# Feed-forwards whose up products read rows not yet normed, with the inverse root multiplied in at the banks

## The chip, the cores and the metric

The kernel runs on one core of a Trainium2 chip. The metric is the device time of one execution in microseconds, the median of several runs. The engines are named as the profile names them: PE (TensorE, matrix products), PEld (its weight loads), DVE (VectorE), ACT (ScalarE), POOL (GpSimd) and SP (SyncE, which issues the weight transfers).

## What is computed

Three residual blocks, one after the other, on 512 rows of width 1024. Each ends in a feed-forward of hidden width 2816 (the second block has two of them). All is float32. The part that matters here:

```python
# first block (second block: silu, centred convolution)
hf = rmsnorm(x, norm_ffn[i])
up = causal_dwconv(hf @ w_up[i], ffn_dw_w[i], ffn_dw_b[i])     # width 3, per channel
gate, val = jnp.split(up, 2, axis=-1)
x = x + (jax.nn.gelu(gate) * val) @ w_down[i]
# third block: no norm ahead, no convolution
ffn = (jax.nn.silu(x @ w_ffn_gate) * (x @ w_ffn_up)) @ w_ffn_down
x = _layernorm(ALPHA * x + ffn, ln2_g, ln2_b)
# rmsnorm(x, g) = x * rsqrt(mean(x * x) + eps) * g, over the width
```

## The kernel before

The residual `G.x` lies in SBUF transposed: 8 tiles (KT) of 128 channels by 512 rows. `feed_forward` (line 210) is called four times: `ffn1`, `ffn2` and `ffn3` with a gain (they norm first) and taps (a convolution of width 3 along the rows), `ffn4` with neither. Every call is a stage of its own: the engines meet before and after it.

**Products.** `exact_product` (line 189) makes a float32 product of three passes over operands split into a rounded high part and the rest as a low part: w_low by x_high, w_high by x_low, w_high by x_high, lines 192 to 194. So both weights and rows have to be split. ACT makes a high part with a copy into fp32r (`high`, line 311, for weights; line 322 for rows), then the low part is the difference: POOL does it for weights (`low`, line 255), DVE for rows (line 365).

**Up part.** Weights come in chunks of 4096 columns per partition through a ring of two slots; a chunk is split in two halves of 2048. A half h of chunk (p, i) gives one gate tile and one value tile of the hidden width, so there are 22 halves, t = 4i + 2p + h. For each half PE does 2 tiles x 8 k x 3 passes = 48 matmuls of 128x512 into two of the eight banks (`up`, line 271): half t uses banks 4p + 2h and the next one, so banks come round again after four halves. `split` counts finished weight halves. The split parts have room for two halves: ACT may make the high part of half t + 2 only when PE is done with half t (`gate_val`), and POOL follows.

**After each half** ACT (lines 324 to 342) first makes that next high part, then two centre taps from the banks with bias (`gc`, `vc`, lines 333 and 335). DVE adds the two side taps to each, reading bank and buffer (line 383, four instructions), ACT applies the activation on the gate (line 338), and DVE multiplies gate by value into `gT` (line 397). The second side taps also set the banks free.

**Entry, with a gain.** `rms_act` (line 144) squares the 8 tiles into `gT`, PE sums them with a matrix of ones into bank 7 (`rms_pe`, 8 products), DVE forms the mean, ACT the root, DVE the reciprocal and the normed rows into `G.hT` (`rms_dve`, lines 166 to 171), ACT and DVE split those 8 tiles, and PE's first product waits for the first of them (`h_split`). Between its squares and the root ACT makes the high parts of halves 0 and 1.

**Down part.** The 22 hidden tiles are split by ACT (line 350) and DVE (line 405) and multiplied with the down weights. Its first product waits for the last bank, for tile 0's split and for the first down weights.

SP loads the next chunk when POOL has split both halves of one (`G.feed` on `split`). `pairs` (line 52) puts the halves of two chunks into one hardware loop on each engine.

## Time and profile before

| | us |
|---|---|
| median of 3 runs | 4812.88 |
| the runs | 4821.88, 4768.9, 4812.88 |
| the profiled execution | 4808.09 |
| its span, first to last instruction | 4806.3 |
| mean granted clock of PE | 0.941 of full speed |

All durations below come from the one profiled execution. A line of the timeline gives the start in us from the span's start, the duration, the engine, the line of the code and, in square brackets, how long the engine sat idle before it and what released it. A line that ends in x8 stands for eight instructions in a row, and its duration is from the start of the first to the end of the last; neighbouring instructions on ACT, DVE and PE overlap a little, so start to start is less than a single duration. Matmul ends are modelled; their starts are what counts.

### The profile page before, as it was taken

What the parts mean: (1) busy time and instruction counts of PE and PEld (TensorE: products, weight loads), DVE (VectorE), ACT (ScalarE), POOL (GpSimd) and SP (SyncE); (2) the same over time, 40 slices, a digit from 0 to 9 for tenths busy, and PEclk for the clock granted to TensorE, in tenths of its full rate; (3) what the DMA queues carried; (4) which work ended last, traced back from release to release, by engine and by line L of the source; (5) the groups of instructions that cost most, each with busy time, mean ns of one, the idle gap of its engine ahead of it and who ended that gap; (6) DMA issues with size and microseconds to landing.
All of it is one profiled execution on the core that took longest, in us unless ns stands there. A gap on an engine that the chain in (4) does not pass through costs nothing. (4 is left out here: it accounts for less than half of the span.)

```text
span 4806.3 us, 55253 instructions
## 1 busy us (share of the span) xinstructions
PE 4393.2 (91%) x22216; PEld 3404.0 (71%) x22216; DVE 2163.0 (45%) x3645; ACT 1362.3 (28%) x2087; POOL 1272.1 (26%) x474
## 2 busy tenths in 40 slices
PE   8999899978989998979999989989998887987998
PEld 6766587734747875668888668757776775765876
DVE  5543333335643345457777533444552436122023
ACT  3343244212203423323333334322222111102222
POOL 1000343301203430000000134334554332653432
PEclk9996999988999999889999999999999998998999
DMA  5200122211112222421000212221211110211221
GB/s 166 105 36 18 70 87 105 92 70 70 70 53 87 98 93 91 158 101 36 21 34 21 72 53 105 88 76 60 81 70 67 60 53 36 88 70 70 103 90 53
DMA packets 41294, 357.92 MB, mean 74 GB/s; under 512 B 4275, under 2 KB 4659, under 8 KB 21500
## 3 DMA queue, kind: packets, MB, share of 16 engines
q1 hardware_dynamic: 41084, 354.97, 20.4%
q8 instruction: 150, 2.46, 0.2%
q14 instruction: 60, 0.49, 0.0%
HBM read 333.46 MB, written 21.50 MB: 74 GB/s over the span
## 5 line engine op out<-in xcount | busy, mean ns | idle before, releaser
L255 POOL TENSOR_TENSOR ffn_weights_low<-weight_ring,ffn_weights_high 128x2048 fp32r<-128x2048 f32 x132 | 615.0, 4660 | 1140.8 <-ACT ffn_weights_high L311 1140.8
L192 PE MATMUL banks<-ffn_in_high,ffn_weights_low 128*128 128x512 f32 x2112 | 829.6, 393 | 92.5 <-DVE ffn_in_low L365 61.8
L193 PE MATMUL banks<-ffn_in_low,ffn_weights_high 128*128 128x512 f32 x2112 | 827.7, 392 | 0.0
L194 PE MATMUL banks<-ffn_in_high,ffn_weights_high 128*128 128x512 f32 x2112 | 826.8, 391 | 0.0
L192 PEld LDWEIGHTS banks<-ffn_in_high,ffn_weights_low 128*128 128x128 f32 x2112 | 400.4, 190 | 181.2 <-issue 67.1
L194 PEld LDWEIGHTS banks<-ffn_in_high,ffn_weights_high 128*128 128x128 f32 x2112 | 400.1, 189 | 84.2
L193 PEld LDWEIGHTS banks<-ffn_in_low,ffn_weights_high 128*128 128x128 f32 x2112 | 400.5, 190 | 83.1
L311 ACT ACTIVATE ffn_weights_high<-weight_ring 128x2048 fp32r<-128x2048 f32 x132 | 252.4, 1915 | 655.4 <-PE banks L194 654.9
L192 PE MATMUL banks<-third_x_high,third_weights_low 128*128 128x512 f32 x832 | 333.5, 401 | 61.5 <-POOL third_weights_low L3011 24.2
L3011 POOL TENSOR_TENSOR third_weights_low<-weight_ring,third_weights_high 128x1024 fp32r<-128x1024 f32 x144 | 361.1, 2508 | 11.5
L3009 POOL CAST third_weights_high<-weight_ring 128x1024 fp32r<-128x1024 f32 x144 | 157.4, 1093 | 653.4 <-PE banks L194 488.2
L193 PE MATMUL banks<-third_x_low,third_weights_high 128*128 128x512 f32 x832 | 329.8, 396 | 0.0
L194 PE MATMUL banks<-third_x_high,third_weights_high 128*128 128x512 f32 x832 | 329.3, 396 | 0.0
L383 DVE SCALAR_TENSOR_TENSOR ffn_gate<-banks,columns_sb,ffn_gate 128x511 f32<-128x511 f32 (+1 forms) x132 | 98.4, 745 | 481.9 <-ACT ffn_value L335 481.9
L2794 POOL TENSOR_TENSOR rwout_weights_low<-weight_ring,rwout_weights_high 128x1024 fp32r<-128x1024 f32 x8 | 18.8, 2384 | 904.0 <-ACT rwout_weights_high L2844 904.0
L405 DVE TENSOR_TENSOR ffn_in_low<-ffn_hidden,ffn_in_high 128x512 fp32r<-128x512 f32 x88 | 172.1, 2004 | 178.7 <-ACT ffn_in_high L350 178.6
L192 PEld LDWEIGHTS banks<-third_x_high,third_weights_low 128*128 128x128 f32 x832 | 160.3, 193 | 99.5 <-DVE third_x_low L3668 17.7
L193 PEld LDWEIGHTS banks<-third_x_low,third_weights_high 128*128 128x128 f32 x832 | 160.1, 192 | 33.7 <-issue 0.7
L194 PEld LDWEIGHTS banks<-third_x_high,third_weights_high 128*128 128x128 f32 x832 | 159.7, 192 | 34.2
L192 PE MATMUL banks<-first_in_high,first_weights_low 128*128 128x512 f32 x336 | 145.8, 434 | 15.5 <-DVE first_in_low L847 12.3
L3262 DVE SCALAR_TENSOR_TENSOR mlstm_conv<-mlstm_z,columns_sb,mlstm_conv 128x512 f32<-128x512 f32 x96 | 134.8, 1404 | 3.4
L193 PE MATMUL banks<-first_in_low,first_weights_high 128*128 128x512 f32 x336 | 136.3, 406 | 0.0
(541 smaller groups left out, 7813.4 us busy)
## 6 DMA issues: line engine op xcount, KB each, us to landing
weight_ring<-weights SPq DMA_DIRECT2D x144, 2048.0 KB, 7.7
scan_in<-rwkv_operands SPq DMA_DIRECT2D x8, 1280.0 KB, 6.6
rwkv_operands<-rwin_staged SPq DMA_DIRECT2D x24, 256.0 KB, 2.1
scan_in<-rwkv_operands SPq DMA_DIRECT2D x8, 512.0 KB, 3.9
bias_tiles<-bias_rows SPq DMA_DIRECT2D x8, 448.0 KB, 9.1
residual<-x SPq DMA_DIRECT2D x4, 512.0 KB, 7.3
filt_decay<-decay SPq DMA_DIRECT2D x1, 2048.0 KB, 8.6
rwkv_residual<-residual SPq DMA_DIRECT2D x1, 2048.0 KB, 7.1
```

Source lines behind the costliest of these rows:

```text
L192: pe.matmul(out, w[1], x[0], start=start, stop=False, skip_group_check=True)
L193: pe.matmul(out, w[0], x[1], start=False, stop=False, skip_group_check=True)
L194: return pe.matmul(out, w[0], x[0], start=False, stop=stop, skip_group_check=True)
L255: pool.tensor_tensor(parts[1], landed, parts[0].bitcast(F32), ALU.subtract).then_inc(S["split"], 1)
L311: act.activation(parts[0], landed, ACT.Copy).then_inc(S["rounded"], 1)
L383: ins = dve.scalar_tensor_tensor(out=buf[:, h, to], in0=G.banks[:, b + q, of], scalar=G.col(taps, 8 * t + 4 * q + tap), in1=buf[:, h, to], ...
L405: dve.tensor_tensor(h_parts[1][:, t % KT, :], gT[:, t, :], h_parts[0][:, t % KT, :].bitcast(F32), ALU.subtract)\
L2794: pool.tensor_tensor(w_parts[1][:, k, :], landed(k), w_parts[0][:, k, :].bitcast(F32), ALU.subtract).then_inc(S["split"], 1)
L3009: pool.tensor_copy(parts[0], landed).then_inc(S["rounded"], 1)
L3011: pool.tensor_tensor(parts[1], landed, parts[0].bitcast(F32), ALU.subtract).then_inc(S["split"], 1)
L3262: ins = dve.scalar_tensor_tensor(out=cv[:, m, :], in0=of, scalar=G.col("m_conv", at + tap), in1=cv[:, m, :], op0=ALU.mult, op1=ALU.add)
```

## The change

In the stages with a gain the up products no longer wait for the norm. They read x times gain, split into high and low; since the inverse root is one number per row, it can be multiplied in after the product. DVE does that for each half: two `tensor_tensor` from the banks by `rstd` into a new SBUF buffer `up_scaled`, and these also set the banks free. Centre taps and side taps then read `up_scaled` instead of the banks. The squares, their sum (now seven additions on DVE and one product with the ones on PE instead of eight), the mean, root and reciprocal run beside the first halves; PE does the one product between the two tiles of half 1. In all four stages the first half's weights are split in eight pieces of 128x256, one per k, in turn with the row tiles; PE takes half 0 with k outside and the two tiles inside, waiting for each piece. Loops of POOL, PE and ACT are cut differently, as half 0 and (on ACT) the first and last chunks stand outside. The diff, its core:

```diff
         gT = G.sb(name + "_hidden", [P, FT, SEQ], ctx=ctx)
-        sq = gT[:, 0:KT, :]
+        sq, square_sum = gT[:, 0:KT, :], gT[:, KT, :]
         rstd = G.sb(name + "_rstd", [P, SEQ], ctx=ctx)
-
+        up_scaled = G.sb(name + "_up", [P, 2, 2, SEQ], ctx=ctx)
         gc = G.sb(name + "_gate", [P, 2, SEQ], ctx=ctx)
         vc = G.sb(name + "_value", [P, 2, SEQ], ctx=ctx)
         w_parts = [G.sb(name + "_weights_" + part, [P, 2, half], F32R, ctx=ctx) for part in ("high", "low")]
-
-        h_parts = [G.sb(name + "_in_" + part, [P, KT, SEQ], F32R, ctx=ctx) for part in ("high", "low")]
-        of = G.x if gain is None else G.hT
+        x_parts = [G.sb(name + "_in_" + part, [P, KT, SEQ], F32R, ctx=ctx) for part in ("high", "low")]
...
+        def pairs_from_one(eng, count, body):
+
+            assert count % 2
+            body(0, 0)
+            with eng.Fori(0, count // 2) as i:
+                body(1, i)
+                body(0, i + 1)
...
                 landed, parts = landed_half(p, h, up)
-                pool.wait_ge(S["rounded"], 4 * i + 2 * p + h + 1)
+                pool.wait_ge(S["rounded"], 4 * i + 2 * p + h)
                 pool.tensor_tensor(parts[1], landed, parts[0].bitcast(F32), ALU.subtract).then_inc(S["split"], 1)
...
+            landed, parts = landed_half(0, 0, True)
+            for k in range(KT):
+                pool.wait_ge(S["piece_high"], k + 1)
+                pool.tensor_tensor(parts[1][:, k, :], landed[:, k, :], parts[0][:, k, :].bitcast(F32), ALU.subtract).then_inc(S["piece_split"], 1)
+            pool.wait_ge(S["piece_split"], KT)
+            pool.sem_inc(S["split"], 1)
+            pairs_from_one(pool, UP_CHUNKS, chunk)
...
+                    t = 4 * i + 2 * p + h
+
+                    def product(m, k):
+                        return exact_product(pe, G.banks[:, 4 * p + 2 * h + m, :], [x[:, k, m * P:(m + 1) * P] for x in w],
+                                             [x[:, k, :] for x in x_parts], start=(k == 0), stop=(k == KT - 1))
+
+                    if first and h == 0:
+                        for k in range(KT):
+                            pe.wait_ge(S["piece_split"], k + 1)
+                            pe.wait_ge(S["x_split"], k + 1)
+                            for m in range(2):
+                                mm = product(m, k)
+                                if k == KT - 1:
+                                    mm.then_inc(S["gate_val"], 1)
+                        continue
+                    pe.wait_ge(S["split"], t + 1)
                     for m in range(2):
-
-                        pe.wait_ge(S["value_free"] if conv and m else S["gate_free"], 4 * i + 2 * p + h + 1)
+                        pe.wait_ge(S["value_scaled"] if m else S["gate_scaled"], t + 1)
+                        if gain is not None and p == h == m == 1:
+                            pe.wait_ge(S["mean_done"], 1)
...
+                            mm = product(m, k)
                         mm.then_inc(S["gate_val"], 1)
-
-            pairs(pe, UP_CHUNKS, up)
+                        if first and gain is not None and m == 0:
+                            pe.wait_ge(S["square_added"], KT - 1)
+                            pe.matmul(G.banks[:, 7, :], G.con("ones"), square_sum, start=True, stop=True).then_inc(S["summed"], 1)
+
...
+            landed, parts = landed_half(0, 0, True)
+            G.arrived(act, 0, 0)
+            for k in range(KT):
+                act.activation(parts[0][:, k, :], landed[:, k, :], ACT.Copy).then_inc(S["piece_high"], 1)
+                if gain is None:
+                    act.activation(x_parts[0][:, k, :], G.x[:, k, :], ACT.Copy).then_inc(S["x_high"], 1)
+                else:
+                    act.activation(x_parts[0][:, k, :], G.x[:, k, :], ACT.Identity, scale=G.col(gain, k)).then_inc(S["x_high"], 1)
+                if k == KT // 2:
+                    high(0, 0, 1, True)
             if gain is not None:
-                rms_act(act, G, S, sq)
-            for h in range(2):
-                high(0, 0, h, True)
-            if gain is not None:
-                rms_root(act, G, S, rstd)
-            for k in range(KT):
-                if gain is not None:
-                    act.wait_ge(S["h_ready"], k + 1)
-                act.activation(h_parts[0][:, k, :], of[:, k, :], ACT.Copy).then_inc(S["h_high"], 1)
+                for k in range(KT):
+                    act.activation(sq[:, k, :], G.x[:, k, :], ACT.Square).then_inc(S["squared"], 1)
 
             def chunk(p, i):
                 for h in range(2):
                     t = 4 * i + 2 * p + h
                     b = 4 * p + 2 * h
-                    act.wait_ge(S["gate_val"], 8 * i + 4 * p + 2 * h + 2)
+                    act.wait_ge(S["gate_val"], 2 * t + 2)
                     high(1 - p, i + p, h, isinstance(i, int) is False or 2 * i + p + 1 < UP_CHUNKS)
+                    if gain is not None and isinstance(i, int) and p == i == h == 0:
+                        rms_root(act, G, S, rstd)
 
                     act.wait_ge(S["hidden"], t + 1)
                     if conv:
-                        act.activation(gc[:, h, :], G.banks[:, b, :], ACT.Identity, bias=G.col(taps, 8 * t + 3),
+                        act.wait_ge(S["gate_scaled"], 4 + t + 1)
+                        act.activation(gc[:, h, :], up_scaled[:, h, 0, :], ACT.Identity, bias=G.col(taps, 8 * t + 3),
                                        scale=G.col(taps, 8 * t + 2 - shift)).then_inc(S["centre"], 1)
-                        act.activation(vc[:, h, :], G.banks[:, b + 1, :], ACT.Identity, bias=G.col(taps, 8 * t + 7),
+                        act.wait_ge(S["value_scaled"], 4 + t + 1)
+                        act.activation(vc[:, h, :], up_scaled[:, h, 1, :], ACT.Identity, bias=G.col(taps, 8 * t + 7),
                                        scale=G.col(taps, 8 * t + 6 - shift)).then_inc(S["centre"], 1)
-                        act.wait_ge(S["gate_free"], 4 + t + 1)
+                        act.wait_ge(S["gate_tapped"], t + 1)
                         act.activation(gc[:, h, :], gc[:, h, :], act_func).then_inc(S["activated"], 1)
                     else:
...
+            chunk(0, 0)
+            with act.Fori(0, UP_CHUNKS // 2 - 1) as i:
+                chunk(1, i)
+                chunk(0, i + 1)
+            chunk(1, UP_CHUNKS // 2 - 1)
+            chunk(0, UP_CHUNKS // 2)
...
+            for k in range(KT):
+                dve.wait_ge(S["x_high"], k + 1)
+                high = x_parts[0][:, k, :].bitcast(F32)
+                if gain is None:
+                    dve.tensor_tensor(x_parts[1][:, k, :], G.x[:, k, :], high, ALU.subtract).then_inc(S["x_split"], 1)
+                else:
+                    dve.scalar_tensor_tensor(out=x_parts[1][:, k, :], in0=G.x[:, k, :], scalar=G.col(gain, k), in1=high,
+                                             op0=ALU.mult, op1=ALU.subtract).then_inc(S["x_split"], 1)
             if gain is not None:
-                rms_dve(dve, G, S, rstd, 7, gain, G.hT)
-            for k in range(KT):
-                dve.wait_ge(S["h_high"], k + 1)
-                dve.tensor_tensor(h_parts[1][:, k, :], of[:, k, :], h_parts[0][:, k, :].bitcast(F32), ALU.subtract).then_inc(S["h_split"], 1)
+                for k in range(1, KT):
+                    dve.wait_ge(S["squared"], k + 1)
+                    if k > 1:
+                        dve.wait_ge(S["square_added"], k - 1)
+                    dve.tensor_tensor(square_sum, sq[:, 0, :] if k == 1 else square_sum, sq[:, k, :], ALU.add).then_inc(S["square_added"], 1)
+                dve.wait_ge(S["summed"], 1)
+                dve.tensor_scalar(rstd[:, :], G.banks[:, 7, :], 1.0 / D, EPS, ALU.mult, ALU.add).then_inc(S["mean_done"], 1)
+                dve.wait_ge(S["root_done"], 1)
+                dve.reciprocal(rstd[:, :], rstd[:, :]).then_inc(S["rstd_done"], 1)
+                dve.wait_ge(S["rstd_done"], 1)
...
+                        for q, free in enumerate((S["gate_scaled"], S["value_scaled"])):
+                            dve.wait_ge(S["gate_val"], 2 * t + q + 1)
+                            dve.tensor_tensor(up_scaled[:, h, q, :], G.banks[:, b + q, :], rstd[:, :], ALU.mult).then_inc(free, 1)
                         dve.wait_ge(S["centre"], 2 * t + 2)
                         for s, (tap, to, of) in enumerate(sides):
                             for q, buf in enumerate((gc, vc)):
                                 if s == 1:
                                     dve.wait_ge(S["tap"], 2 * t + q + 1)
                                 ins = dve.scalar_tensor_tensor(
-                                    out=buf[:, h, to], in0=G.banks[:, b + q, of], scalar=G.col(taps, 8 * t + 4 * q + tap),
+                                    out=buf[:, h, to], in0=up_scaled[:, h, q, of], scalar=G.col(taps, 8 * t + 4 * q + tap),
                                     in1=buf[:, h, to], op0=ALU.mult, op1=ALU.add)
                                 if s == 0:
                                     ins.then_inc(S["tap"], 1)
                                 else:
-                                    ins.then_inc((S["gate_free"], S["value_free"])[q], 1)
+                                    ins.then_inc((S["gate_tapped"], S["value_tapped"])[q], 1)
                         dve.wait_ge(S["activated"], t + 1)
-                        dve.wait_ge(S["value_free"], 4 + t + 1)
-                        value = vc[:, h, :]
+                        dve.wait_ge(S["value_tapped"], t + 1)
+                        dve.tensor_tensor(gT[:, t, :], gc[:, h, :], vc[:, h, :], ALU.mult).then_inc(S["hidden"], 1)
...
```

## Rows read from the trace of the kernel before

**Rows 1.** The page, busy time of each engine over the whole span

```profile
PE 4393.2 (91%) x22216; PEld 3404.0 (71%) x22216; DVE 2163.0 (45%) x3645; ACT 1362.3 (28%) x2087; POOL 1272.1 (26%) x474
```

**Rows 2.** Timeline, PE and ACT, entry of `ffn1`: start us, us, engine, line

```profile
558.89 0.39 PE L194 MATMUL banks<-first_in_high,first_weights_high 128*128 128x512 f32 x1
560.30 4.27 ACT L147 ACTIVATE ffn_hidden<-residual 128x512 f32<-128x512 f32 x8 [43.54 <-PEq L1106]
...
581.42 0.77 PE L192 MATMUL banks<-ffn_in_high,ffn_weights_low 128*128 128x512 f32 x1 [13.31 <-DVE ffn_in_low L365]
```

**Rows 3.** Timeline, ACT, POOL and DVE between those rows

```profile
564.47 3.70 ACT L311 ACTIVATE ffn_weights_high<-weight_ring 128x2048 fp32r<-128x2048 f32 x2
566.45 9.04 POOL L255 TENSOR_TENSOR ffn_weights_low<-weight_ring,ffn_weights_high 128x2048 fp32r<-128x2048 f32 x2 [14.43 <-ACT ffn_weights_high L311]
568.16 0.69 DVE L166 TENSOR_SCALAR ffn_rstd<-banks 128x512 f32<-128x512 f32 x1 [8.15 <-PE banks L159]
569.48 0.63 ACT L152 ACTIVATE ffn_rstd<-ffn_rstd 128x512 f32<-128x512 f32 x1
570.15 3.35 DVE L168 RECIPROCAL ffn_rstd<-ffn_rstd 128x512 f32<-128x512 f32 x1 [1.30 <-ACT ffn_rstd L152]
573.54 2.50 DVE L171 SCALAR_TENSOR_TENSOR normed<-residual,columns_sb,ffn_rstd 128x512 f32<-128x512 f32 x1
```

**Rows 4.** Timeline, ACT, its first instruction after halves 0, 1 and 3

```profile
594.10 1.28 ACT L311 ACT_TABLE_LOAD   x1 [12.76 <-PE banks L194]
...
604.92 1.92 ACT L311 ACTIVATE ffn_weights_high<-weight_ring 128x2048 fp32r<-128x2048 f32 x1 [3.38 <-PE banks L194]
...
626.68 1.92 ACT L311 ACTIVATE ffn_weights_high<-weight_ring 128x2048 fp32r<-128x2048 f32 x1 [4.64 <-PE banks L194]
```

**Rows 5.** Timeline, all engines, last up half of `ffn1` to first down product

```profile
822.09 0.39 PE L194 MATMUL banks<-ffn_in_high,ffn_weights_high 128*128 128x512 f32 x1
822.51 1.91 ACT L311 ACTIVATE ffn_weights_high<-weight_ring 128x2048 fp32r<-128x2048 f32 x1 [4.87 <-PE banks L194]
...
824.50 4.57 POOL L255 TENSOR_TENSOR ffn_weights_low<-weight_ring,ffn_weights_high 128x2048 fp32r<-128x2048 f32 x1 [6.20 <-ACT ffn_weights_high L311]
...
825.79 0.75 DVE L383 SCALAR_TENSOR_TENSOR ffn_gate<-banks,columns_sb,ffn_gate 128x510 f32<-128x510 f32 x1 [6.95 <-ACT ffn_value L335]
...
827.89 0.63 ACT L338 ACTIVATE ffn_gate<-ffn_gate 128x512 f32<-128x512 f32 x1 [2.13 <-DVE ffn_gate L383]
...
828.62 1.00 DVE L397 TENSOR_TENSOR ffn_hidden<-ffn_gate,ffn_value 128x512 f32<-128x512 f32 x1
...
830.32 0.76 PE L192 MATMUL banks<-ffn_in_high,ffn_weights_low 128*128 128x512 f32 x1 [7.84 <-issue]
```

**Rows 6.** Timeline, entry of `ffn4`, ACT, POOL and DVE

```profile
4386.55 3.71 ACT L311 ACTIVATE ffn_weights_high<-weight_ring 128x2048 fp32r<-128x2048 f32 x2 [0.28 <-PEq L3700]
...
4393.06 5.08 POOL L255 TENSOR_TENSOR ffn_weights_low<-weight_ring,ffn_weights_high 128x2048 fp32r<-128x2048 f32 x1
4393.57 5.12 DVE L365 TENSOR_TENSOR ffn_in_low<-residual,ffn_in_high 128x512 fp32r<-128x512 f32 x1
...
4422.65 1.92 ACT L311 ACTIVATE ffn_weights_high<-weight_ring 128x2048 fp32r<-128x2048 f32 x1 [5.69 <-PE banks L194]
```

**Rows 7.** One line's instructions: duration ns min/median/max, forms

```profile
L1131 POOL TENSOR_TENSOR first_weights_low<-weight_ring,first_weights_high x8: 2372/2429/2430, 482.7 to 549.6; 128x1024 fp32r<-128x1024 f32 x8
```

**Rows 8.** Timeline, PE, first product after an idle time of 2.41 and 4.25 us

```profile
155.79 0.50 PE L192 MATMUL banks<-first_in_high,first_weights_low 128*128 128x512 f32 x1 [2.41 <-DVE first_weights_low L872]
...
4152.16 0.77 PE L192 MATMUL banks<-third_x_high,third_weights_low 128*128 128x512 f32 x1 [4.25 <-DVE third_x_low L3668]
```

**Rows 9.** Timeline, DVE and POOL in the first stage of the kernel

```profile
28.21 3.69 DVE L847 TENSOR_TENSOR first_in_low<-normed,first_in_high 128x512 fp32r<-128x512 f32 x6
...
28.77 5.43 POOL L622 TENSOR_TENSOR first_weights_low<-weight_ring,first_weights_high 128x1024 fp32r<-128x1024 f32 x1 [6.87 <-ACT first_weights_high L751]
```

**Rows 10.** The page, costliest groups: busy us, mean ns of one, idle before

```profile
L3262 DVE SCALAR_TENSOR_TENSOR mlstm_conv<-mlstm_z,columns_sb,mlstm_conv 128x512 f32<-128x512 f32 x96 | 134.8, 1404 | 3.4
```

40 lines of the change are left out of this document (17 added, 23 removed).

## Prediction

> **What bounds the kernel now.** First the busy times of the page: PE works 91% of the span [rows 1], so a change pays only where it closes a gap of PE or shortens its stream. Next the timeline of PE where a feed-forward begins: the last product of the stage before starts at 558.89 and the first up product at 581.42 [rows 2]; only the eight products with the ones lie between. That is 22.5 us of mostly idle PE; from ACT's first instruction, 560.30, to that product it is 21.1 us, and `ffn2` and `ffn3` repeat this within 0.1 us, two entries more of the same kind. Third, what fills it [rows 3]: squares, two high parts of weights, mean (568.16), root (569.48), reciprocal (570.15, 3.35 us), then the normed rows from 573.54, then their split. Fourth, when halves end: ACT is free and waits for PE, so its first instruction after a half marks the end: 594.10, 604.92, 626.68 for halves 0, 1 and 3 [rows 4]. A half at full rate takes (626.68 - 604.92) / 2 = 10.9 us, 0.226 us for each of 48 matmuls; half 0 takes 12.7, the 1.8 us more being the low clock after a long idle time. Last the joint to the down part, 822.09 to 830.32 [rows 5]: another gap, in which a chain over ACT, POOL and DVE sets the end.
>
> **The port, which decides most of this.** At 573.54 DVE starts an instruction with two SBUF inputs that takes 2.50 us [rows 3]; POOL's subtraction, also two SBUF inputs, ends at 566.45 + 9.04 = 575.49, and DVE 0.55 later. The same in `ffn4`: 5.12 us for a subtraction [rows 6]. But the side tap at 825.79, with one input in a bank, takes 0.75 us in the middle of POOL's 4.57 [rows 5]. So a DVE instruction with both tensors in SBUF waits for POOL's to end, and one that reads a bank does not. The change moves the side taps' source from banks to SBUF and adds seven additions of that kind. The Trainium skill, SBUF — State Buffer, section "Who interferes with whom", says that a DVE instruction with two SBUF inputs blocks against a GpSimd one that reads SBUF, for the whole instruction, which speaks against such a move; the trace agrees (2.50 us beside 0.75). Taken as bandwidth shared or as nothing, the sum would be rival C's; taken as a lock it is the one below.
>
> **Entry of ffn1 to ffn3, from ACT's first instruction (0 = 560.30 [rows 2]).** Before: first product 21.1, half 0 ends 33.8, half 1 44.6, half 3 66.4 [rows 2, 4].
>
> Half 0. ACT now alternates a piece of 128x256 and a row tile. 512 columns take 0.53 from start to start (4.27 / 8, [rows 2]) and 2048 take 1.85 (3.70 / 2, [rows 3]), so 256 take 0.3, a pair 0.9, and eight pairs with half 1's high part 9.1 us: ACT isn't the limit. A POOL piece isn't in the trace: 1024 columns take 2.43 [rows 7], 2048 take 4.57 [rows 5], so a straight line through the two gives 0.8 for 256, which I take; bounds are 0.57 (an eighth of 4.57) and 1.2 (half of 2.43). The low part of the rows is DVE with two SBUF inputs, 0.66. Both want the port, so a pair costs 0.8 + 0.66 and some 0.1 for handing over, 1.56 us, against 6 x 0.226 = 1.36 of PE. First product at 2.0, last pair ready at 0.45 + 12.5 = 12.9, half 0 done at 14.3 to 14.7 (the latter with 1.8 us of low clock).
>
> Half 1. Its low part follows the pieces on POOL: 13.6 to 18.2 (one addition may come ahead). PE waits for it some 3.5 us, then takes the gate tile, 18.3 to 23.7. Meanwhile DVE has seven additions, each with two SBUF inputs and each waiting for the one before, so POOL can take the port between any two. I expect one before POOL's 4.6 us, one between that and the next low part (half 2's, 18.9 to 23.5), five after it at 0.75: done at 27.3. PE stands from 23.7, does the ones product at 27.4 and the value tile to 33.3. After an idle time of 2.41 us the first product takes 0.50, after 4.25 us 0.77 [rows 8], the low clock again: 1.5 us more, 34.8. Half 2 ends 45.7.
>
> Half 3 needs its weights, and here a wait is added: ACT makes their high part only after the root and after half 0's taps. The chain: mean 28.1 to 28.7, root 29.4, reciprocal 32.8 (0.69, 0.63, 3.35 [rows 3]), two multiplications from the banks 34.1 (0.69 each as the mean, which also reads a bank, no port), centre taps 34.9, three side taps 37.0, activation 37.6, high part 39.5, POOL 44.2. That is ahead of 45.7, so it costs nothing; half 3 ends at 56.6 in place of 66.4. Gain 9.8 us in each of three stages, 29.4 us. Of the 19 us by which the first product comes earlier, half is lost again to the port.
>
> **The middle of the up part.** Each half now puts two more DVE instructions of 0.69 from the banks, under ACT's high part of 1.91, so hidden. From the half's end: POOL done at 824.50 + 4.57 - 822.51 = 6.6, side taps wait for that, second gate tap done 6.6 + 0.55 + 2 x 0.66 = 8.5, activation 9.1, plus 1.3 for a table load in one half of four. PE gives 10.9. Cover is 1.8 us (0.5 with the load), so nothing is lost; without the cover each us costs 20 halves x 3 = 60 us. DVE's work for a half, 1.4 + 2.8 + 0.8, is far under 10.9. SP's loads move with `split`, two chunks ahead, hidden.
>
> **Joint to the down part, ffn1 to ffn3.** Behind the taps stand the last hidden product and then the split of tile 0. Before, the hidden product starts at 828.62 and ends at 829.62, and PE starts at 830.32 [rows 5]. After, POOL ends at 829.07 as now, the first tap at 829.6, three more by 831.6, the hidden product at 832.5: 2.9 us later, 8.7 us in three stages. PE is idle long enough to have the low clock either way.
>
> **Entry of ffn4.** No norm, no taps, only the pieces. Before, from 4386.55: DVE's second subtraction waits 5.12 us for POOL's second [rows 6], half 1 ends at 36.1. After: pairs of 0.8 + 0.6 (3.69 / 6, [rows 9]) + 0.1, done at 12.5, half 1's low part at 17.1, half 1 ends at 17.2 + 10.9 = 28.1. Gain 8.0 us.
>
> **Sum.** 29.4 - 8.7 + 8.0 = 28.7 us. Against the profiled execution, 4808.1, that gives 4779.4, taken as **4779 us**. The median of the runs is 4812.9, 5 us above that execution, and the runs spread over 53 us, so the sum is less than their spread. A measurement of this kernel can tell about 1%, 48 us, from no change.
>
> **Rivals.**
> A, the sum above: 0.5.
> B, DVE keeps the port. In the first stage POOL's instruction at 28.77 takes 5.43 us in place of 2.4, waiting out five DVE subtractions issued after it [rows 9]. The Trainium skill, SBUF — State Buffer, section "Who interferes with whom", has it that issue order decides who blocks; this trace goes beyond it, as later ones went ahead. If the last six additions run like this once half 1's low part is done, they end at 22.5, PE never waits for them and keeps its clock, half 1 ends at 29.6, half 2 at 40.5, half 3's weights are just ready (POOL 40.5) and it ends at 51.5. Gain 14.9 a stage, sum 44, 4764 us. For it: the rows; against it: those subtractions didn't wait for one another. Chance 0.2.
> C, no port trouble: PE starts at 1.8, half 1's low part done 14.3, additions hidden, half 3 ends 47.4, gain 19.0; ffn4 11.0; no loss at the joint: 68 us, 4740. Rows 3 and 6 speak against it: 0.05.
> D, the other side: the chain of a half becomes the bound. It has 1.8 us of cover. If every tap and the hidden product took the 1404 ns that a three-tensor DVE instruction beside POOL takes on average [rows 10], instead of one wait at the start, the second gate tap would end at 6.6 + 3 x 1.4 = 10.8, the activation at 11.4: 0.5 to 0.6 beyond, 33 us lost, and the kernel is 4 us slower, 4812; at 1 us beyond, 31 us slower, 4839. It decides from 0.5 us beyond PE's 10.9. Against it: that mean holds waits for whole POOL instructions, which the wait to 6.6 already counts. Chance 0.06.
> E, small pieces are dear. At 1.2 us for a piece a pair costs 1.96, half 1 starts 3.2 later in four stages, 12.8 us: sum 15.9, 4792. With 0.57 it's 7.4 us better, 4772. The dear side: 0.15.
> The rest, 0.04, is that the entry gains nothing because something else of the stage is late.
>
> **How the numbers follow.** A, B and E hold 0.85 and span 4764 to 4792; the runs' own spread adds some 12 us on both sides: range 4750 to 4806. Faster by over 1% needs 48 us: C and half of B with the spread, and a tail of A: 0.18. Slower by over 1% is D at its dear end: 0.03. Within 1%: 0.79.
>
> **What would show it.** Right: first up product 2 us after ACT's first instruction; POOL pieces and row subtractions in turn, 1.5 to 1.6 us a pair; a PE wait for the low part of half 1 and another for the additions; side taps of which the first of a half takes about 3 us and ends 0.5 us after POOL; PE without gaps from half 4 to 21; a joint of 10.7 to 11 us in place of 7.84. Wrong: gaps of PE at every half (D); additions that end before the gate tile (B); first taps of 0.75 us beside POOL (C); pieces over 1 us (E).

## The result, and the profile after

| | before | after |
|---|---|---|
| median, runs of one comparison | 4774.32 us (11 runs) | 4742.32 us (11 runs) |
| ratio after / before, from all runs (the medians give 0.9933) | | 0.9928, interval 0.9899 to 0.9958 |
| span of the profiled execution | 4806.3 us | 4736.5 us |
| mean granted clock of PE | 0.941 | 0.951 |

The change makes the kernel 32 us faster by the medians, 0.7%. The prediction had 28.7 us (ratio 4779 / 4812.9 = 0.993) and "within 1%", so the size of the change came out nearly as forecast. The time itself did not: 4742 lies 37 us under 4779 and 8 us below the range. The two statements fit together only if the kernel before is itself faster than 4812.9, and that is where the error sits.

The page's row of PE's granted clock, in tenths, one digit for each fortieth of the span, before and then after:

```profile
PEclk9996999988999999889999999999999998998999
```

```profile
PEclk9999999979999999889999999989998998989999
```

The fourth digit, 6 against 9, covers 361 to 481 us: code that the change does not touch. Stretches of the trace of before, all engines (columns: us; then busy us and count of PE, PEld, DVE, ACT, POOL; granted clock; DMA share; GB/s):

```profile
403.70:552.10 148.40, 145.62 (x461) 98.42 (x462) 43.10 (x139) 33.60 (x86) 27.60 (x16) 0.71 0.12 43
404.00:479.00 75.00, 74.91 (x217) 51.37 (x218) 21.62 (x104) 20.39 (x63) 0.00 (x0) 0.50 0.08 29
```

and the same stretch of code (the last part of the attention and the stage from it to `ffn1`) in the trace of after:

```profile
408.30:519.30 111.00, 107.85 (x453) 73.93 (x453) 41.77 (x134) 32.22 (x82) 27.72 (x16) 0.98 0.16 57
```

For 75 us, in the attention's part, PE was granted half speed, the lower of its two levels (1.2 GHz) in place of 2.4, and was busy all the time. The stretch took 148.4 us there and 111.0 after: 37.4 us of the 69.8 between the two spans belong to that one execution.

The duration of each feed-forward (for `ffn2` with its neighbours) is what the change can move. It is counted between the points where POOL, which is through first, ends its work in a stage. Each column is one profiled execution, in us; "before again" is an experiment below.

| | before | before again | after | gain, second to third |
|---|---|---|---|---|
| the front, ahead of the attention | 228.6 | 227.5 | 232.8 | -5.3 |
| the attention's last part and the stage after it | 148.4 | 109.7 | 111.1 | -1.4 |
| `ffn1` | 384.8 | 385.5 | 377.0 | 8.5 |
| `ffn2` | 509.7 | 509.2 | 502.1 | 7.1 |
| `ffn3` | 435.8 | 436.6 | 428.6 | 8.0 |
| `ffn4` | 397.2 | 395.8 | 385.9 | 9.9 |

The four feed-forwards give 33.5 us (33.9 against the first column), where the sum had 28.7. Ahead of `ffn4` POOL's point lies 24.1 or 25.8 us before PE's last product, by execution, so the row of `ffn4` carries up to 1.7 us of that. Counted on PE, from its last product ahead of the stage to its last in it, `ffn4` takes 395.0, 395.2 and 385.4 us: 9.6 to 9.8 less. Where this count reads `ffn4` otherwise below, it is given as "on PE".

Now the steps. The timeline of after, entry of `ffn1`, PE, ACT, POOL and DVE (start us, us, engine, line; in brackets idle before and releaser); ACT's first instruction starts at 527.51, which is 0 in the text:

```profile
526.10 0.39 PE L194 MATMUL banks<-first_in_high,first_weights_high 128*128 128x512 f32 x1
529.05 1.18 POOL L271 TENSOR_TENSOR ffn_weights_low<-weight_ring,ffn_weights_high 128x256 fp32r<-128x256 f32 x1
529.78 0.47 PE L192 MATMUL banks<-ffn_in_high,ffn_weights_low 128*128 128x512 f32 x1 [3.30 <-DVE ffn_in_low L405]
530.19 1.20 POOL L271 TENSOR_TENSOR ffn_weights_low<-weight_ring,ffn_weights_high 128x256 fp32r<-128x256 f32 x1
531.34 1.20 POOL L271 TENSOR_TENSOR ffn_weights_low<-weight_ring,ffn_weights_high 128x256 fp32r<-128x256 f32 x1
...
534.40 0.75 POOL L271 TENSOR_TENSOR ffn_weights_low<-weight_ring,ffn_weights_high 128x256 fp32r<-128x256 f32 x1 [0.70 <-ACT ffn_weights_high L342]
...
537.67 4.87 POOL L260 TENSOR_TENSOR ffn_weights_low<-weight_ring,ffn_weights_high 128x2048 fp32r<-128x2048 f32 x1 [0.18 <-POOL ffn_weights_low L271]
537.96 5.13 DVE L412 TENSOR_TENSOR ffn_hidden<-ffn_hidden 128x512 f32<-128x512 f32 x1
543.20 5.01 DVE L412 TENSOR_TENSOR ffn_hidden<-ffn_hidden 128x512 f32<-128x512 f32 x1
549.11 0.69 DVE L412 TENSOR_TENSOR ffn_hidden<-ffn_hidden 128x512 f32<-128x512 f32 x1
552.25 2.07 PE L309 MATMUL banks<-ffn_hidden,constants_sb 128*128 128x512 f32 x2 [3.92 <-DVE ffn_hidden L412]
553.33 1.42 PE L192 MATMUL banks<-ffn_in_high,ffn_weights_low 128*128 128x512 f32 x1
```

PE's empty time between the stages shrinks from 22.5 us [rows 2] to 3.7 (526.10 to 529.78). Pieces on POOL start every 1.15 us and show 1.18 to 1.20 each, since the wait for the port stands inside an instruction's duration; the one at 534.40, which starts after both engines have waited for ACT, shows 0.75. The first addition (537.96) starts just after POOL's low part of half 1 (537.67) and ends just after it, though an addition without POOL beside it takes 0.69 (549.11); the second does the same beside half 2's low part. PE has nothing from the gate tile's end to 552.25 and comes out of it with the low clock: the row of two instructions, one product with the ones, takes 2.07 us and the next matmul 1.42.

A half in the middle, timeline of after, POOL and DVE:

```profile
575.56 4.69 POOL L260 TENSOR_TENSOR ffn_weights_low<-weight_ring,ffn_weights_high 128x2048 fp32r<-128x2048 f32 x1 [4.42 <-ACT ffn_weights_high L337]
577.11 3.67 DVE L438 SCALAR_TENSOR_TENSOR ffn_gate<-ffn_up,columns_sb,ffn_gate 128x510 f32<-128x510 f32 x1 [1.34 <-ACT ffn_value L368]
580.71 0.74 DVE L438 SCALAR_TENSOR_TENSOR ffn_value<-ffn_up,columns_sb,ffn_value 128x510 f32<-128x510 f32 x1
```

The first side tap waits for POOL to end and then runs its own 0.7; the second, with POOL idle, takes 0.74. PE shows no gap in halves 4 to 21.

The joint to the down part of `ffn1`, timeline of after:

```profile
778.24 1.91 ACT L337 ACTIVATE ffn_weights_high<-weight_ring 128x2048 fp32r<-128x2048 f32 x1 [1.66 <-PE banks L194]
780.23 4.52 POOL L260 TENSOR_TENSOR ffn_weights_low<-weight_ring,ffn_weights_high 128x2048 fp32r<-128x2048 f32 x1 [6.18 <-ACT ffn_weights_high L337]
781.60 3.69 DVE L438 SCALAR_TENSOR_TENSOR ffn_gate<-ffn_up,columns_sb,ffn_gate 128x510 f32<-128x510 f32 x1 [2.66 <-ACT ffn_value L368]
...
787.38 0.69 DVE L447 TENSOR_TENSOR ffn_hidden<-ffn_gate,ffn_value 128x512 f32<-128x512 f32 x1
788.78 0.77 PE L192 MATMUL banks<-ffn_in_high,ffn_weights_low 128*128 128x512 f32 x1 [10.57 <-issue]
```

Beside [rows 5]: the tap 3.69 in place of 0.75, PE's gap 10.57 in place of 7.84.

When halves end, from ACT's first instruction, in us (the start of a half's last matmul plus 0.226, which is up to 0.3 ahead of the mark by ACT that [rows 4] gives):

| `ffn1` | first product | half 0 | half 1 | half 2 | half 3 |
|---|---|---|---|---|---|
| before | 21.1 | 33.5 | 44.4 | 55.3 | 66.2 |
| predicted | 2.0 | 14.3 to 14.7 | 34.8 | 45.7 | 56.6 |
| after | 2.3 | 13.3 | 32.7 | 43.6 | 54.7 |

`ffn1` is the best of the four at its start. In `ffn2`, `ffn3` and `ffn4` half 0 ends at 14.9, 16.0 and 15.8 (the first product of `ffn3` comes at 3.4), because PE has part of the half in its low clock: granted clock 0.87, 0.87 and 0.80 over half 0, where `ffn1` has 1.00. In the two with a norm that costs nothing by itself, as the additions are awaited until 24.7 and 25.2 there, 24.7 in `ffn1`; half 1 ends at 34.1 and 33.1, the 34.1 with more of the low clock behind the ones product (0.68 granted over 9.6 us).

### The profile page after: what moved, and what is told of

Its sections match the earlier page's. It is cut to its first block and busy times, and to the rows that moved or that the text cites. A ratio compares the mean times of both kernels' runs of the same rounds, so it can differ in the third digit from the quotient of the medians.

```text
span 4736.5 us, 55353 instructions
## 1 busy us (share of the span) xinstructions
PE 4343.9 (92%) x22174; PEld 3377.4 (71%) x22174; DVE 2453.9 (52%) x3774; ACT 1322.5 (28%) x2079; POOL 1295.0 (27%) x502
## 5 line engine op out<-in xcount | busy, mean ns | idle before, releaser
L260 POOL TENSOR_TENSOR ffn_weights_low<-weight_ring,ffn_weights_high 128x2048 fp32r<-128x2048 f32 x128 | 601.2, 4697 | 824.5 <-ACT ffn_weights_high L337 823.8
L438 DVE SCALAR_TENSOR_TENSOR ffn_gate<-ffn_up,columns_sb,ffn_gate 128x511 f32<-128x511 f32 (+1 forms) x132 | 287.2, 2176 | 167.6 <-ACT ffn_value L368 167.6
L3063 POOL TENSOR_TENSOR third_weights_low<-weight_ring,third_weights_high 128x1024 fp32r<-128x1024 f32 x144 | 363.2, 2522 | 11.5
L193 PEld LDWEIGHTS banks<-third_x_low,third_weights_high 128*128 128x128 f32 x832 | 159.7, 192 | 33.5 <-issue 0.7
L194 PEld LDWEIGHTS banks<-third_x_high,third_weights_high 128*128 128x128 f32 x832 | 158.9, 191 | 33.9
L371 ACT ACTIVATE ffn_gate<-ffn_gate 128x512 f32<-128x512 f32 x66 | 41.8, 633 | 334.0 <-DVE ffn_gate L438 334.0
```

The source lines that it names most:

```text
L193: pe.matmul(out, w[0], x[1], start=False, stop=False, skip_group_check=True)
L194: return pe.matmul(out, w[0], x[0], start=False, stop=stop, skip_group_check=True)
L260: pool.tensor_tensor(parts[1], landed, parts[0].bitcast(F32), ALU.subtract).then_inc(S["split"], 1)
L371: act.activation(gc[:, h, :], gc[:, h, :], act_func).then_inc(S["activated"], 1)
L438: ins = dve.scalar_tensor_tensor(out=buf[:, h, to], in0=up_scaled[:, h, q, of], scalar=G.col(taps, 8 * t + 4 * q + tap), in1=buf[:, h, to] ...
L3063: pool.tensor_tensor(parts[1], landed, parts[0].bitcast(F32), ALU.subtract).then_inc(S["split"], 1)
```

## Experiments

Durations of a stage are compared between single profiled executions. The same program repeats them within 1.5 us (after and after again, below), so differences from 2 us on are read, and only as a pattern over stages. "Fewer" and "more" are against after unless said otherwise.

### Was the base disturbed? (before_again)

The kernel before, unchanged.

> The kernel before, unchanged, profiled once more. Theory 1: the 37.4 us by which the attention-to-merge stage between 403.7 and 552.1 us of the first profile was longer than in the changed kernel is a stretch of low granted clock (0.50) that belongs to that one execution. Then this stage takes about 111 us here, the span is near 4770, and the four feed-forward stages still take what they took (384.8, 509.7 with its neighbours, 435.8, 397.2 us between the meetings of engines). Theory 2: it belongs to the code before the change (placement, memory layout), and the changed kernel cured it: then it takes about 148 us again.

Measured 4762.34 us, span 4760.5 (near 4770 expected). The stretch that took 148.4:

```profile
401.50:512.20 110.70, 107.40 (x458) 73.30 (x458) 42.63 (x137) 32.94 (x87) 28.66 (x17) 1.00 0.16 58
```

Clock 1.00 and 109.7 us between POOL's points, while the feed-forwards repeat within 1.4 us. The slow stretch was that execution's, not the kernel's. In four comparisons the kernel before ran 64 times: 53 runs lie between 4763 and 4782, the other 11 above 4800; two of the three runs shown ahead of the prediction were of the rare kind. Runs of after have the same tail (4776.81, 4786.89 and 4799.53 among 21).

### The side taps' source (banks)

DVE scales the banks in place; taps and centre taps read the banks again, which are now free only after the taps.

```diff
-dve.tensor_tensor(up_scaled[:, h, q, :], G.banks[:, b + q, :], rstd[:, :], ALU.mult)
+dve.tensor_tensor(G.banks[:, b + q, :], G.banks[:, b + q, :], rstd[:, :], ALU.mult)
-out=buf[:, h, to], in0=up_scaled[:, h, q, of], ...
+out=buf[:, h, to], in0=G.banks[:, b + q, of], ...
```

> The changed kernel, but DVE writes the scaled values back into the banks instead of up_scaled, centre and side taps read the banks, and the banks are set free by the second side taps again. So side taps have one SBUF input again, with the same work otherwise. Port theory: side taps take 0.75 us beside POOL in every half; at the joint to the down part PE's gap falls from 10.57 to about 7.9 us in ffn1 to ffn3, 2.7 us each, 8 us in all, and ffn4 stays. The middle of the up part keeps its pace (a half 10.9 us). Rival, the joint is longer because of the two more multiplications: the gap stays at 10.5 us.

4738.11 us, ratio to before 0.9945 (0.9903 to 0.9987). Timeline, joint of `ffn1`:

```profile
773.22 4.58 POOL L259 TENSOR_TENSOR ffn_weights_low<-weight_ring,ffn_weights_high 128x2048 fp32r<-128x2048 f32 x1 [6.20 <-ACT ffn_weights_high L338]
774.51 0.75 DVE L442 SCALAR_TENSOR_TENSOR ffn_gate<-banks,columns_sb,ffn_gate 128x510 f32<-128x510 f32 x1 [2.58 <-ACT ffn_value L369]
779.05 0.77 PE L192 MATMUL banks<-ffn_in_high,ffn_weights_low 128*128 128x512 f32 x1 [7.85 <-issue]
```

The tap is back at 0.75 in the middle of POOL's instruction, the gap back at 7.85 (before 7.84). `ffn1` to `ffn3` take 2.7, 3.1 and 3.0 us less, 8.8 in sum; `ffn4`, which has no taps, takes 387.3 against 385.9 and 387.4 in two executions of after (385.2 against 385.4 and 385.2 on PE). So the joint's loss is the port, and nothing else. The median of all runs does not resolve 9 us.

### What stands ahead of the down part (late)

ACT makes the high part for the down part's second weight half not before the last taps but after the first two hidden tiles; POOL's low part, which keeps the port from the taps, follows it.

```diff
-high(1 - p, i + p, h, ...)
+if not (last and h):
+    high(1 - p, i + p, h, ...)
...
 for t in range(FT):
+    if t == 2:
+        high(1, UP_CHUNKS // 2, 1, False)
```

> The changed kernel, but ACT makes the high part of the second down weight half after the split of hidden tile 1 instead of ahead of the last half's taps, so POOL's subtraction isn't running when the last taps and the first tile splits want the port. Port theory: at the joint only the chain of last multiplication, centre taps, side taps, activation, hidden product and tile split is left: PE's gap 6 us in place of 10.57 in ffn1 to ffn3, and about 3 us in place of 7.2 in ffn4: 13.5 + 4 = 17 to 18 us faster than the changed kernel. Rival, the chain of taps itself sets the joint: the gap falls by no more than ACT's 1.9 us, to 8.7. A new wait may show up 11 us after the joint, where the second down weight half is needed: expected none, with 2 us to spare.

4726.14 us, the median of 4722.35, 4722.37, 4729.91 and one execution of 9856.77, which stays unexplained and is left out of the ratio: 0.989 (0.9815 to 0.9964). Timeline, `ffn1`:

```profile
784.39 1.89 ACT L337 ACTIVATE ffn_weights_high<-weight_ring 128x2048 fp32r<-128x2048 f32 x1
784.94 0.77 PE L192 MATMUL banks<-ffn_in_high,ffn_weights_low 128*128 128x512 f32 x1 [5.84 <-issue]
786.36 4.64 POOL L260 TENSOR_TENSOR ffn_weights_low<-weight_ring,ffn_weights_high 128x2048 fp32r<-128x2048 f32 x1 [11.45 <-ACT ffn_weights_high L337]
```

The gap is 5.84 (2.48 in `ffn4`, from 7.22), with POOL's work now behind PE's start, and no new gap opens where that half is wanted. The stages take 5.7, 4.2, 4.3 and 5.6 us less (7.2 in `ffn4` on PE), 19.8 in sum. That agrees with the joint read as a chain of ACT's high part, the port and the taps.

### Eight products with the ones in place of the additions (pesum)

PE sums the squares after half 0 as before the change; the seven additions on DVE are gone.

```diff
+if gain is not None:
+    rms_pe(pe, G, S, sq, 7)
...
-if first and gain is not None and m == 0:
-    pe.wait_ge(S["square_added"], KT - 1)
-    pe.matmul(G.banks[:, 7, :], G.con("ones"), square_sum, ...)
```

> The changed kernel, but the sum of squares is made as before the change, by eight products with the ones on PE, right after half 0, and DVE's seven additions are gone. PE then works in the wait for half 1's low part (1.64 us), and the additions no longer queue for POOL's port. Port theory: the 5.0 us gap in half 1 and the low clock behind it vanish; PE pays 3.4 us less 1.6 instead: 4 to 5 us faster in each of three stages, 12 to 15 us in all. Rival, the additions were late because ACT's squares were late: the gap moves ahead of half 1 and the gain is under 2 us a stage.

4741.61 us, ratio 0.9932 (0.991 to 0.9954). A miss: the stages take 2.6 and 0.8 us less and 0.6 more. Timeline, PE, `ffn1`:

```profile
542.11 7.03 PE L159 MATMUL banks<-ffn_hidden,constants_sb 128*128 128x512 f32 x16
548.58 0.79 PE L192 MATMUL banks<-ffn_in_high,ffn_weights_low 128*128 128x512 f32 x1
```

The wait for the additions did vanish, but the sum's eight products are 16 PE instructions and take 7.03 us, twice the 3.4 that the expectation had. They are float32, not fp32r: the sixteenth starts at 548.55, so from start to start a product costs 0.86 us where a pass of an up product costs 0.226. Half 1's products begin at about 20 instead of 17. The kernel before could have told: its same eight products start at 560.98, and the mean, which waits for the last of them, at 568.16 [rows 3]. The Trainium skill, FP8 and Floating Point Precision, section "TensorE Precision Notes", has true FP32 as four passes through the array; 0.86 / 0.226 = 3.8 agrees in time, and that the profile lists each product as two instructions is this trace's.

### No pieces (whole)

Half 0's weights in one piece on ACT and POOL, ahead of the row tiles.

```diff
-for k in range(KT):
-    pool.wait_ge(S["piece_high"], k + 1)
-    pool.tensor_tensor(parts[1][:, k, :], landed[:, k, :], ...)
+low(p, i, h, True)
```

> The changed kernel without the pieces: the first half's weights are split whole (one high part, one low part) in all four feed-forwards; the norm is still applied after the products. Theory: POOL's first low part then runs from 2.0 to 6.6 us after ACT's first instruction and the rows' first low part waits for it, first product at 7.3 in place of 2.3; the other row splits queue with half 1's low part. In ffn4 nearly all of the gain goes (half 1 ends at about 36 us in place of 26.6, 9 to 10 us slower than the changed kernel), since pieces are its only change; in ffn1 to ffn3 only some 2 us a stage, since half 1's low part and the additions are then no longer late. Rival, the norm taken off the path gives most by itself and pieces little everywhere: under 3 us in ffn4 too.

4748.31 us in one run. Timeline, entry of `ffn1`:

```profile
521.84 4.57 POOL L260 TENSOR_TENSOR ffn_weights_low<-weight_ring,ffn_weights_high 128x2048 fp32r<-128x2048 f32 x1 [10.27 <-ACT ffn_weights_high L330]
522.41 12.21 DVE L396 SCALAR_TENSOR_TENSOR ffn_in_low<-residual,columns_sb,ffn_in_high 128x512 fp32r<-128x512 f32 x6 [2.85 <-ACT ffn_in_high L337]
527.11 0.76 PE L192 MATMUL banks<-ffn_in_high,ffn_weights_low 128*128 128x512 f32 x1 [8.28 <-DVE ffn_in_low L396]
```

First product at 7.3, as expected, 5 us later than with pieces, since DVE's first row split waits for the whole of POOL's instruction. Of the six in that row the first takes 4.55 us and the second, beside half 1's low part, 5.08; the others 0.74. In `ffn4` half 1 ends at 32.7, 6.1 us later than with pieces, where 36 was expected, and the stage takes 8.0 us more (6.3 on PE), not 9 to 10: a miss in size, though far from the rival's 3. In `ffn1` half 0 ends 11.4 us later (24.7 against 13.3), yet half 3 only 4.4, and `ffn1` to `ffn3` take 4.4, 0.0 and 3.9 more, 8.3 in sum where some 6 were expected. In a stage with a norm most of what the pieces win ahead is lost again at the additions.

### How much cover a half has (double_after, double_before)

POOL does each up half's low part twice, with a wait between; the second writes the same values. Once on the kernel after, once on the kernel before.

```diff
+if up:
+    pool.tensor_tensor(parts[1], landed, parts[0].bitcast(F32), ALU.subtract).then_inc(S["extra"], 1)
+    pool.wait_ge(S["extra"], 4 * i + 2 * p + h)
 pool.tensor_tensor(parts[1], landed, parts[0].bitcast(F32), ALU.subtract).then_inc(S["split"], 1)
```

> The changed kernel with POOL's subtraction of each up half done twice (the first eight pieces excepted), the same result. Port theory: the chain of a half is high part 1.97, POOL 9.5, then side taps up to the second gate tap 1.9, activation 0.65: 14.0 us against PE's 10.9, so PE gets a gap of about 3 us in nearly every half of ffn1 to ffn3, some 60 us a stage, and about 0.6 us a half, 12 us, in ffn4, which has no taps. Without a lock on the taps ffn1 to ffn3 would lose as little as ffn4.

> The kernel before with POOL's subtraction of each up half done twice, the same result. The partner of the doubled changed kernel: here the side taps read banks and don't wait for POOL, so only POOL's own time counts: high part 1.97 and POOL 9.5 against PE's 10.9, 0.6 us a half, about 12 us in each of the four stages. If ffn1 to ffn3 lose here as much as in the doubled changed kernel, the taps' port has nothing to do with it.

4940.06 and 4888.75 us, one run each. Timeline of the kernel after with the doubled low part, one half of `ffn1`:

```profile
612.00 4.70 POOL L261 TENSOR_TENSOR ffn_weights_low<-weight_ring,ffn_weights_high 128x2048 fp32r<-128x2048 f32 x1 [3.76 <-ACT ffn_weights_high L340]
613.54 3.71 DVE L441 SCALAR_TENSOR_TENSOR ffn_gate<-ffn_up,columns_sb,ffn_gate 128x510 f32<-128x510 f32 x1 [1.32 <-ACT ffn_value L371]
616.77 4.96 POOL L263 TENSOR_TENSOR ffn_weights_low<-weight_ring,ffn_weights_high 128x2048 fp32r<-128x2048 f32 x1
617.16 5.12 DVE L441 SCALAR_TENSOR_TENSOR ffn_value<-ffn_up,columns_sb,ffn_value 128x510 f32<-128x510 f32 x1
621.79 0.50 PE L192 MATMUL banks<-ffn_in_high,ffn_weights_low 128*128 128x512 f32 x1 [2.32 <-POOL ffn_weights_low L263]
```

and of the kernel before:

```profile
590.32 4.67 POOL L256 TENSOR_TENSOR ffn_weights_low<-weight_ring,ffn_weights_high 128x2048 fp32r<-128x2048 f32 x1 [3.72 <-ACT ffn_weights_high L314]
591.74 0.75 DVE L386 SCALAR_TENSOR_TENSOR ffn_gate<-banks,columns_sb,ffn_gate 128x510 f32<-128x510 f32 x1 [9.66 <-ACT ffn_value L338]
595.07 4.99 POOL L258 TENSOR_TENSOR ffn_weights_low<-weight_ring,ffn_weights_high 128x2048 fp32r<-128x2048 f32 x1
600.11 0.50 PE L192 MATMUL banks<-ffn_in_high,ffn_weights_low 128*128 128x512 f32 x1 [1.04 <-POOL ffn_weights_low L258]
```

With 4.7 us more on POOL the taps of after wait twice and PE stands 2.3 us in each half (3 expected): `ffn1` to `ffn3` take 59.4, 61.5 and 62.2 us more (60 expected), `ffn4`, without taps, 14.8 or, on PE, 13.4 (12). The same load on before costs 30.7, 29.9, 30.4 and 32.3 us (30.7 in `ffn4` on PE) against before again. That is a miss, 12 expected: some 8.7 us is the entry (first product at 29.8 in place of 21.1), which the expectation forgot, the rest gaps of 2.27 and 1.04 us in every four halves. But its taps take 0.745 us throughout. So the half of after stands on a chain through the port that before did not have: it is hidden at POOL's 4.6 us, and its cover is under 4.7. An estimate from the rows: in the doubled kernel a half comes every 13.5 us in place of 10.9, so 4.8 us more (616.77 - 612.00) cost 2.6, which leaves about 2.2 of cover, where the prediction had 1.8.

### Two cuts together (both)

`late` and `pesum` in one kernel.

> The changed kernel with the sum of squares on PE after half 0 and the late high part at the joint, both together. The two touch different places, so their gains add: 12 to 15 and 17 to 18 us, some 30 us faster than the changed kernel, 60 us (1.3%) faster than the kernel before. If they share a cause (PE's clock, or the same chain), the sum is clearly under 25 us.

4726.65 us, ratio 0.9869 (0.9818 to 0.9921). The stages take 6.7, 6.5, 4.6 and 5.6 us less, 23.4 in sum, about what the two gave alone (19.8 and 2.8); the front of this build took 0.5 more. Short of the 30 expected, by `pesum`'s miss.

### Does after repeat itself? (after_again)

The kernel after, unchanged.

> The changed kernel, unchanged, once more. In its first profile the first stage, whose code the change doesn't touch, takes 232.8 us, and 227 to 229 in five other kernels of this study (the kernel before among them), 233 to 234 in three. Theory 1: that is chance of an execution, as the low clock stretch was: about 228 this time in one of two. Theory 2: it goes with the program as built: 232 to 234 again, and 5 to 6 us of the change's gain are lost there for as long as it is built like this. The feed-forward stages repeat within 1.5 us either way.

4739.0 us, ratio 0.9947 (0.991 to 0.9985). The feed-forwards repeat within 1.5 us, the front takes 231.5 (232.8 before it), where the two executions of the kernel before show 228.6 and 227.5. The difference of some 4 us in code that no edit touches seems to go with the build more than with chance, as far as two executions of each tell; over all builds the front takes 226.9 to 235.7 us. What of the build it is stays open.

### The ones product behind the value tile (order)

The additions get until the value tile is done; ACT first makes the high part of half 3, then the root.

```diff
-if first and gain is not None and m == 0:
+if first and gain is not None and m == 1:
     pe.wait_ge(S["square_added"], KT - 1)
...
+if start and h == 0:
+    act.wait_ge(S["gate_val"], 4)
+    high(1, 0, 1, True)
     rms_root(act, G, S, rstd)
```

> The changed kernel with one step of the start reordered in ffn1 to ffn3: PE does the value tile of half 1 before the one product with the ones, and ACT makes half 3's high part before the root instead of behind the first half's taps. The additions then have half 1's whole 10.9 us to finish. Port theory: the 5.0 us gap and the low clock behind it (1.6 us) go; half 1 ends at 26.0 in place of 32.6 after ACT's first instruction, but the root's chain now starts 1 us later and ACT's backlog makes half 4's weights 2 us late, a new gap; net 3.5 to 4.5 us a stage, 11 to 13 us in all. Rival, the backlog on ACT takes all of it back: gaps at halves 4 and 5 sum to 6 us and the stages stay as they are.

4733.43 us, ratio 0.991 (0.9885 to 0.9936). Timeline, PE, `ffn1`:

```profile
556.60 1.02 PE L309 MATMUL banks<-ffn_hidden,constants_sb 128*128 128x512 f32 x2
...
582.09 0.71 PE L192 MATMUL banks<-ffn_in_high,ffn_weights_low 128*128 128x512 f32 x1 [2.66 <-POOL ffn_weights_low L260]
```

PE reaches the ones product without idle time and with its clock, so it takes 1.02 us in place of 2.07. Half 1 ends at 26.1 in place of 32.7, but half 4 waits for its weights: 2.66 us here, 1.28 in `ffn2` and `ffn3`. The high part of that half now stands behind the root and the delayed taps of half 0. Behind the longer wait comes the low clock (0.87 granted from 582.0 to 594.7, 1.00 in the same half of `ffn2`), some 1.7 us more in `ffn1`, which gains least. That leaves 2.3, 5.6 and 4.0 us less, 11.9 in sum, the 11 to 13 expected.

### The cuts that worked (best, best_banks)

`best` is `order` with `late`; `best_banks` has the taps on the banks as well.

> The changed kernel with the reordered start and the late high part at the joint, both together. Gains add: 11 to 13 us and the 19.8 us that the late high part gave in the four stages, 31 us less than the changed kernel, about 1.5% under the kernel before.

> The same as the one with both reorderings, and the scaled values kept in the banks as well, so that side taps never wait for POOL. With the late high part nothing runs on POOL at the joint, so the banks' 2.7 us a stage should not come again there; at the start the taps' chain gets shorter by up to 3 us only in halves that lie behind PE. Expected: within 2 us a stage of the kernel without it. If it gains 8 us more, the port costs something in the middle of the up part after all.

The first three rows are of one comparison, in which after is `after_again`; the last row has `before_again`, the first profile of after, and the two new ones.

| | before | after | best | best_banks |
|---|---|---|---|---|
| us, median | 4774.5 | 4739.0 | 4708.75 | 4708.49 |
| ratio to before | | 0.9947 | 0.9897 | 0.9884 |
| interval | | 0.991 to 0.9985 | 0.9837 to 0.9957 | 0.9809 to 0.9958 |
| `ffn1` / `ffn2` / `ffn3` / `ffn4` | 385.5 / 509.2 / 436.6 / 395.8 | 377.0 / 502.1 / 428.6 / 385.9 | 370.7 / 491.8 / 419.2 / 380.3 | 370.6 / 491.7 / 419.6 / 380.3 |

`best` takes 31.6 us less than after in its feed-forwards (31 expected), span 4705.9. Four of its six runs lie between 4705.8 and 4709.6, below every one of the 21 runs of after (4732.4 and up). Two others (4752.7, 4766.8) had the same kind of tail as above; they widen the interval and pull the ratio up, where the medians alone give 0.9862. So `best` stands below after by its median and its stages; the ratios alone, whose intervals overlap, don't separate the two. `best_banks` is the same within 0.4 us a stage: once the joint has no POOL instruction beside the taps and halves have cover, the taps' port costs nothing more that these stages show.

## Why the prediction was right in size and wrong in level

**The base: wrong, and this alone put the time out of the range.** The step was "Against the profiled execution, 4808.1, that gives 4779.4", with the runs' spread added as 12 us on both sides. That execution held 37.4 us too much in a stretch at clock 0.71, which no part of the argument touched. 4808.1 less 37.4 less 28.7 is 4742.0, and 4742.3 was measured. That it comes so close is partly luck, since some 5 us more gain in the feed-forwards stood against 4 to 7 us of loss in the front and the stage after the attention. The three runs shown were themselves a warning: 4768.9 apart from 4812.9 and 4821.9 is two groups, not a spread around a middle.

**The port, as a lock: right.** The first tap of a half, with both tensors in SBUF, takes 3.67 and 3.69 us beside POOL in the rows shown; one that reads a bank takes 0.75 in the same place of the same program but for its source (`banks`). Rival C is out. The Trainium skill, SBUF — State Buffer, section "Who interferes with whom", has a DVE instruction with two SBUF inputs contend with one of GpSimd that reads SBUF; these rows agree.

**Entry, half 0: right in kind, one term too dear.** In `ffn1` the first product came at 2.3 (2.0 predicted) and half 0 ended at 13.3 (14.3 to 14.7); in the other three it ended at 14.9 to 16.0, with part of the half in the low clock, for which the 14.7 stood. The mis-sized term is the pair: 1.56 us predicted, 1.15 measured. Its parts were about right: a piece that does not wait shows 0.75 (0.8 taken), a row split likewise 0.75 (0.66 taken). Their addition was not, for the sum of the two durations is more than the time from one pair to the next: an instruction holds the other off for less than the duration that it shows. [rows 3] had shown that already, where DVE ended 0.55 us after POOL though such an instruction shows 0.69 or more. In `ffn4`, with DVE on its own splits beside them, all eight pieces take 8.85 us, 1.11 each:

```profile
4327.39 8.85 POOL L271 TENSOR_TENSOR ffn_weights_low<-weight_ring,ffn_weights_high 128x256 fp32r<-128x256 f32 x8 [36.95 <-ACT ffn_weights_high L342]
```

So half 1's gate tile started at 15.1 (542.59 - 527.51), not 18.3. The prediction's sign for E, "pieces over 1 us", did appear, as 1.18 to 1.20; it was a poor sign, since these durations hold the wait for the port. What E stood on, a pair of 1.96 us, did not, and E is out.

**The additions: right in kind and count.** One waited beside half 1's low part (5.13 us), one beside half 2's (5.01), five ran at about 0.7 after them, done at 24.7 where 27.3 was predicted. In `ffn3` three came between the two that waited (5.17 and 4.96 us), and they were done at 25.2. B, DVE keeping the port, is out. In `ffn1` POOL's instruction starts ahead of the addition beside it both times (537.67 and 537.96, 542.98 and 543.20). In `ffn3` it starts at 2757.32, in the middle of an addition, and takes 4.80 us, while the next addition, at 2757.71, waits for it; in [rows 9] five subtractions went ahead of POOL. That the wait of each addition for the last lets POOL in is the likely reading; no run changes that wait alone. PE stood idle for 3.92 us (3.7 predicted), and the low clock followed it (0.80 granted over the next 8.1 us). From the start of the ones product (24.7) to the end of half 1 (32.7) it was 8.0 us against the 7.4 of the sum (27.4 to 34.8), since that product is two PE instructions, 2.07 us in the low clock; in `ffn2` it was 9.4. Half 3 came 11.5, 10.8 and 11.1 us earlier in `ffn1` to `ffn3`, against 9.8; its weights were never late.

**The middle: right.** No gap in halves 4 to 21, D is out. In the half shown the first tap ended 0.53 us after POOL (0.55 taken from [rows 3]). `double_after` showed the chain to be real, since 4.7 us more on POOL made it the bound.

**The joint: right.** 2.9 us predicted, 2.73 measured in `ffn1` (10.57 - 7.84), and `banks` took it back.

**`ffn4`: right, slightly under.** Half 1 ended at 26.6 (28.1 predicted) by the cheaper pair; on PE the stage gained 9.6 to 10.0 us over two executions of each kernel, against 8.0.

**What the sum had no term for.** The front of the kernel and the stretch from the attention to `ffn1` took some 4 to 7 us more in both executions of after, in unchanged code. That this belongs to the build is what two executions each suggest; its cause was not tried.

## What to carry to other kernels

When two instructions take turns at a port, a pair is priced from where they start and end in a trace, since their durations overlap and may hold a wait. Before a sum is set against one profiled execution, the granted clock is read over the whole span, and a stretch of low clock with a fully busy PE in code that the change does not touch is taken out of the base. When two engines share a port, an operand moved into SBUF is priced by the instruction of the other engine that runs beside it, and its cure can be the order (what stands ahead of the chain) as well as the operand. Work brought forward at an entry is worth only what the next wait leaves of it, so the chain behind it (here additions, one product, root) is what to cut next.

## What the runs showed of the hardware

A busy PE can be granted half speed for a long stretch in one execution and not in the next: 0.50 over 75 us, with PE 74.91 us busy, then 1.00 over the same code. A product of 128x512 in plain float32 is two PE instructions and 0.86 us from start to start, and after 3.92 us of idle time such a one takes 2.07. A wait for the port stands in the profile as part of the instruction that waits, on POOL (1.19 against 0.75 for a piece) as on DVE (5.13 against 0.69 for an addition); and POOL and DVE in turn need less than the sum of their lone durations, 1.15 us for a pair of 0.75 and 0.75. One engine's wait for the port does not depend on issue order alone: five subtractions issued after POOL's went ahead of it [rows 9], while in `ffn3` POOL came in the middle of a chain of additions and had the port next.
